# Gate products of a dense expert stage run on GpSimd between its row transfers instead of on VectorE

## The chip, the cores and the metric

One core of a Trainium2 chip runs the whole kernel, one launch. The metric is the device time in microseconds (us) of one execution; lower is better. TensorE multiplies matrices, VectorE and ScalarE work elementwise, GpSimd here issues DMA transfers and does a little elementwise work, SyncE only issues DMA.

## What is computed

Two layers of a diffusion backbone over 512 latent and 256 context tokens of width 1024. Each layer has a mixing part and then an expert part ("PEER"). Only the expert part is touched by the change:

```
def block(args):
    hb, eb, gb = args
    a = jnp.einsum('td,tkd->tk', hb, u_tab[eb])
    w = gb.astype(hb.dtype) * jax.nn.gelu(a, approximate=False)
    return jnp.einsum('tk,tkd->td', w, v_tab[eb])
```

Every token picks 128 of 16384 experts. Expert e has a row u and a row v; its gate times gelu(h . u) weights v in the output. The product `gb * gelu(a)` is what the change moves, for the tokens that are treated densely.

## The kernel before

It does the expert part in two ways at once. **Dense**: for most tokens (512 in layer 0, 384 in layer 1) it computes h . u for *all* 16384 experts as matmuls and multiplies by a gate matrix that is zero where a token didn't pick the expert. **Gathered**: for the remaining tokens (two groups of 128 in layer 0, one in layer 1) it fetches the picked rows of u and v by indirect DMA, 128 rows of 4 KB (one for each token) at a time, and treats them on VectorE.

The experts come in 128 tiles of 128, two tiles c = 0, 1 per *step* s, `NSUPER` = 64 steps a layer. fp32 accuracy is had by splitting each operand in a high and a low part (fp32r) and doing three matmuls for each product. In one step:

- TensorE does `apply_u` for step s+1 (48 matmuls, tile 0 and then tile 1, into PSUM banks psA 0 and 1) and then `apply_v` for step s (48 matmuls: four resident accumulators in psV, and four output chunks of 12 matmuls in turn, "cycled" through psA banks 2 and 3). The next step's `apply_u` follows. It waits for `hi_done` and `lo_done` (both parts of an expert tile's weights), for `w_ready` (both parts of the activations W) and for `cycled_free` (a cycled bank emptied).
- ScalarE takes gelu of u's result into `gel` (`gelu(c, s)`), then, after the product with the gates, makes `W_hi` (`high(c, s)`), and makes `split_hi` of the expert tiles.
- VectorE, in an order written out by hand in `experts`: `product(c, s)` (gel times gates, in place), `low(c, s)` (`W_lo` = gel - W_hi), `split_one` (`split_lo` of an expert tile, four a step: the two v tiles of this step, then the two u tiles of step s+2), `add_cycled(q)` (adds a cycled bank into xT), and `rows_used` (the work on one gathered transfer: for u a multiply with a sum, L1925, for v a multiply and add into y_tok, L1930). `share` is the number of such row ops a step: 8 in layer 0, 4 in layer 1.
- GpSimd issues the gathers (`gather(u)`, L1012) into a ring of 7 buffers (`RING`) and once a step the load of the gate block for step s+2 (`load_gates`, L1002) into one of two slots. A gather waits until VectorE has used the row that was in its buffer; the gates load waits until both `W_lo` of the step are made (`w_ready`), since then the slot is read out.
- SyncE loads the expert tiles, 512 KB each, into four `raw` buffers; a load waits until both parts of the tile four back are split.

`gel` has one buffer for each c: `gelu(c, s+1)` waits for `low(c, s)`. Engines go through their own order strictly, so whatever stands behind a wait waits too.

Of the kernel before, what the change touches and what calls it, by code (L numbers as in the profile page):

```python
# [34 lines left out]
ALU = mybir.AluOpType  # L35
# [9 lines left out]
TB = 32  # L45
# [9 lines left out]
NSUPER = NK // 2  # L55
# [9 lines left out]
DENSE = ((NCTX, NLAT), (NCTX, NLAT - P))  # L65
# [10 lines left out]
def gate_blocks(layer):  # L76

    s, n = DENSE[layer]
    return s // TB, (s + n) // TB
# [48 lines left out]
def build_program(nc, mod_pairs, mod_tiles, tiles, x_in, consts, params, bmod, cond, arow, aws, bw, keys, lblog, rope, pu0, pu1, pv0, pv1, gates, out):  # L128
    sem_ctx = ExitStack()

    def semaphore(name):
        return sem_ctx.enter_context(nc.semaphore(name))
# [14 lines left out]
    product_ready = semaphore("product_ready")  # L147
# [4 lines left out]
    g_landed = (semaphore("g_landed0"), semaphore("g_landed1"))  # L152
# [76 lines left out]
    gelu_ready = semaphore("gelu_ready")  # L229
# [34 lines left out]
    def in_r(name, offset, shape, dt=F32):  # L264
        assert offset + int(np.prod(shape[1:])) * 4 <= nc.sbuf_usable_end - RB, name
        return place(name, shape, dt, RB + offset)
# [103 lines left out]
    gel = in_r("gel", 16384, [P, 2, NLAT])  # L370
    g_in = in_r("g_in", 20480, [P, 2, NLAT // TB, 2 * TB])
# [23 lines left out]
    def pick(l, u):  # L395

        part, j = PASSES[l][u // PICKS]
        return part, j, u % PICKS
# [540 lines left out]
    @block.gpsimd  # L939
    def _(pool):  # L940
        seen = Counts()
        for k in range(KD):
            pool.dma_start(xT[:, k, :], x_in[:, k, :]).then_inc(inputs_landed, 16)
        for dst, src in ((cst[:], consts), (par[:], params), (bm[:], bmod), (c_raw[:], cond), (lb[:, 0:2, :], lblog)):
            pool.dma_start(dst, src).then_inc(inputs_landed, 16)

        def a_weights(l):
            pool.dma_start(a_wsT[:], aws[l]).then_inc(aw_landed, 16)
            pool.dma_start(a_bias[:], arow[l, :, 0:256]).then_inc(aw_landed, 16)
            pool.dma_start(a_norm[:], arow[l, :, 256:512]).then_inc(aw_landed, 16)  # L950

        a_weights(0)
        for b in range(2):

            seen.n[g_stored[b]] = 16
        for l in range(DEPTH):

            pool.wait_ge(a_done, seen.upto(a_done))
            pool.memset(states[:], 0.0).then_inc(states_zero, 1)
            pool.wait_ge(c_done, seen.upto(c_done))  # L960
            pool.dma_start(bc[64:96], rope).then_inc(rope_landed, 16)
            pool.dma_start(w_uq[:], bw[l]).then_inc(bw_landed, 16)
            pool.wait_ge(mix_ready, seen.upto(mix_ready))
            pool.dma_start(keysT[:], keys[l]).then_inc(keys_landed, 16)

            tb0, tb1 = gate_blocks(l)
            pool.wait_ge(sel_copied, seen.upto(sel_copied, DENSE[l][1] // P))
            if l + 1 < DEPTH:
                a_weights(l + 1)
            base = 3 + l * (NLAT // TB) * GROUPS  # L970
            steps = (tb1 - tb0) // 2 - 1
            nc.gpsimd.tensor_copy(first_key[:, 0], idxT[:, 0, tb0 * TB + 2:tb0 * TB + 4]).then_inc(pool_chain, 1)

            def first_one_hots(i, last):

                for g in range(2 * GROUPS):

                    pool.wait_ge(oh_passed, seen.at(oh_passed, base + g - 2 + (2 * GROUPS * steps if last else 0)))
                    pool.wait_ge(pool_chain, seen.upto(pool_chain))
                    if not last:  # L980
                        t = i * (2 * TB) + (tb0 * TB + 4 * (g + 1) + 2)
                        nc.gpsimd.tensor_copy(first_key[:, (g + 1) % 4], idxT[:, 0, bass.ds(t, 2)]).then_inc(pool_chain, 1)
                    elif g < 2 * GROUPS - 1:
                        t = (tb1 - 2) * TB + 4 * (g + 1) + 2
                        nc.gpsimd.tensor_copy(first_key[:, (g + 1) % 4], idxT[:, 0, t:t + 2]).then_inc(pool_chain, 1)
                    for j in range(2):
                        ins = nc.gpsimd.tensor_scalar(onehot[:, g % 4, 0, 2 + j], iota, first_key[:, g % 4, j:j + 1], None,  # L987
                                                      ALU.is_equal)
                    ins.then_inc(oh_first, 1)

            with pool.Fori(0, steps) as i:
                seen.enter(i, {oh_passed: 2 * GROUPS, pool_chain: 2 * GROUPS})
                first_one_hots(i, False)
            seen.leave(steps)
            first_one_hots(None, True)

            for b in range(2):
                pool.wait_ge(g_stored[b], seen.upto(g_stored[b], 16 * (tb1 - tb0) // 2))

            def load_gates(s, slot):  # L1000

                return pool.dma_start(g_in[:, slot, 0:tb1 - tb0, :].rearrange("p b (i t) -> p b i t", i=2),  # L1002
                                     gates[tb0:tb1].rearrange("b p (s i) t -> s p b i t", i=2)[s])\
                    .then_inc(g_landed[slot], 16)

            def gather(u):

                part, j, e = pick(l, u)
                b = (UNIT0[l] + u) % RING
                if UNIT0[l] + u >= RING:  # L1010
                    pool.wait_ge(row_used, UNIT0[l] + u - RING + 1)
                nc.gpsimd.indirect_dma_start(rows[:, b, :], None, ((pu0, pv0), (pu1, pv1))[l][part],  # L1012
                                             bass.IndirectOffsetOnAxis(pick_i[:, j, e:e + 1], 0))\
                    .then_inc(rows_landed[b], 16)

            load_gates(0, 0)
            load_gates(1, 1)
            pool.wait_ge(picked, seen.upto(picked, len(GATHERED[l])))
            share = UNITS[l] // NSUPER
            for s in range(NSUPER):  # L1020
                for u in range(s * share, (s + 1) * share):
                    gather(u)
                pool.wait_ge(w_ready, seen.upto(w_ready, 2))
                if s + 2 < NSUPER:
                    load_gates(s + 2, s % 2)
        pool.wait_ge(x_ready, seen.upto(x_ready, 1 + 2 * DEPTH))
        pool.dma_start(out, xT[:, :, NCTX:T]).then_inc(out_stored, 16)
        pool.wait_ge(out_stored, 16)
# [392 lines left out]
    def _(dve):  # L1421
        seen = Counts()
        seen.n[psum_V_free] = 4
        V = nc.vector
# [456 lines left out]
        def experts(l):  # L1881
            s0, n = DENSE[l]
            unit = [0]
            share = UNITS[l] // NSUPER

            def product(c, s):

                dve.wait_ge(gelu_ready, 2 + (l * NSUPER + s) * 2 + c + 1)
                if c == 0:
                    dve.wait_ge(g_landed[s % 2], seen.upto(g_landed[s % 2], 16))  # L1890
                g3 = gel[:, c, 0:n].rearrange("p (b t) -> p b t", t=TB)
                V.tensor_tensor(g3, g3, g_in[:, s % 2, 0:n // TB, c * TB:(c + 1) * TB], ALU.mult).then_inc(product_ready, 1)  # L1892

            def low(c, s):

                dve.wait_ge(whi_ready, seen.upto(whi_ready))
                V.tensor_tensor(W_lo[:, s % 2, c, 0:n], gel[:, c, 0:n], W_hi[:, s % 2, c, 0:n].bitcast(F32),  # L1897
                                ALU.subtract).then_inc(w_ready, 1)
# [33 lines left out]

            extra = share == 8
            dve.wait_ge(htok_ready, seen.upto(htok_ready))
            product(0, 0)
            low(0, 0)
            split_to(EX0[l] + 4)
            for s in range(NSUPER):
                base = splits[0]
                product(1, s)  # L1940
                rows_used(1)
                low(1, s)
                split_to(min(base + 1, EX0[l] + EXPERT_TILES))
                if extra:
                    rows_used(1)
                split_to(min(base + 2, EX0[l] + EXPERT_TILES))
                if s + 1 < NSUPER:
                    product(0, s + 1)
                rows_used(1)
                if s + 1 < NSUPER:  # L1950
                    low(0, s + 1)
                if extra:
                    rows_used(1)
                add_cycled(0)
                rows_used(1)
                add_cycled(1)
                split_to(min(base + 3, EX0[l] + EXPERT_TILES))
                if extra:
                    rows_used(1)
                add_cycled(2)  # L1960
                rows_used(1)
                split_to(min(base + 4, EX0[l] + EXPERT_TILES))
                if extra:
                    rows_used(1)
                add_cycled(3)
# [209 lines left out]
```

## Time and profile before

| | us |
|---|---|
| median of 3 runs | 5521.78 (5520.38 to 5523.92) |
| the profiled execution's own time | 5521.46 |
| its span, first to last instruction | 5519.6 |
| busy: TensorE / VectorE / ScalarE / GpSimd | 4585.9 / 3738.2 / 1635.1 / 1408.4 |
| expert stage of layer 0 | about 1814 to 3233 |
| expert stage of layer 1 | about 4422 to 5511 |
| granted TensorE clock, mean of the span | 0.872 of full speed |

Busy time says how much of the span an engine's instructions cover. For an end-to-end time one asks which wait ends last in a stage; an engine's idle time matters only if the others wait for what it does next. In the timelines a row's first number is the start from the span's start, the second the busy time, the third the engine, and a bracket tells how long the engine had been idle before and what ended it. The busy times of neighbours can overlap by some hundredths, so the place that an instruction takes in an engine's order is the difference of two starts.

### The profile page before, as it was taken

The page shows a single profiled execution, that of the slowest core. Times are in us where ns is not written, and L with a number is a line of the kernel's source. Part 1 is how long each engine was busy: PE and PEld are TensorE (multiplying, and loading weights), DVE is VectorE, ACT ScalarE, POOL GpSimd, SP SyncE. Part 2 cuts the span into 40 slices and gives each one's busy share as a digit, 9 for nine tenths or more (in the row PEclk, how much of TensorE's full clock was granted, in tenths as well). Part 3 has the DMA queues.
Part 4 walks back from the last instruction along what each step waited for, and adds up shares of the span by engine and source line. Part 5 has one row for each costly group of instructions (what it writes and reads, how often), then busy time and mean ns, then how long its engine had stood idle before and what let it go on. Part 6 is the DMA issues. An engine that isn't in the chain of part 4 may idle for free. (4 is left out here: it accounts for less than half of the span.)

```text
span 5519.6 us, 73901 instructions
## 1 busy us (share of the span) xinstructions
PE 4585.9 (83%) x24885; PEld 3932.6 (71%) x24885; DVE 3738.2 (68%) x7426; ACT 1635.1 (30%) x2249; POOL 1408.4 (26%) x1600
## 2 busy tenths in 40 slices
PE   5956599988627999999999978557782799999998
PEld 4956377776516788888888857534462699999998
DVE  1157322235999788889989952733469978888887
ACT  1221233322114322322322322234420333333332
POOL 0000000000029544544444410000000933333332
PEclk9965577779859999999999989568796999999999
DMA  3100022221104899999999931000010377778876
GB/s 123 58 1 1 15 84 84 84 88 35 39 35 175 286 316 312 313 317 311 314 315 311 314 117 39 1 15 0 20 65 23 166 254 281 275 271 280 278 270 230
DMA packets 232170, 898.96 MB, mean 163 GB/s; under 512 B 26160, under 2 KB 26192, under 8 KB 226656
## 3 DMA queue, kind: packets, MB, share of 16 engines
q0 software_dynamic: 129440, 474.96, 25.2%
q1 hardware_dynamic: 102528, 421.57, 21.6%
q8 instruction: 94, 1.54, 0.1%
q14 instruction: 108, 0.88, 0.1%
HBM read 835.61 MB, written 60.82 MB: 162 GB/s over the span
## 5 line engine op out<-in xcount | busy, mean ns | idle before, releaser
L414 PE MATMUL psA<-h_hi,split_hi 128*128 128x512 f32 (+2 forms) x2816 | 1017.5, 361 | 109.4 <-DVE h_lo L1452 64.6
L414 PE MATMUL psA<-h_lo,split_hi 128*128 128x512 f32 (+2 forms) x2816 | 1013.2, 360 | 0.0
L414 PE MATMUL psA<-h_hi,split_lo 128*128 128x512 f32 (+2 forms) x2816 | 1012.9, 360 | 0.0
L1434 DVE TENSOR_TENSOR split_lo<-raw,split_hi 128x1024 fp32r<-128x1024 f32 x596 | 727.2, 1220 | 225.8 <-ACT split_hi L1046 215.8
L1046 ACT ACTIVATE split_hi<-raw 128x1024 fp32r<-128x1024 f32 x596 | 629.9, 1057 | 90.8 <-PE psV L414 76.2
L414 PEld LDWEIGHTS psA<-h_hi,split_hi 128*128 128x128 f32 x2816 | 532.8, 189 | 172.7 <-DVE h_lo L1452 66.3
L1361 ACT ACTIVATE W_hi<-gel 128x512 fp32r<-128x512 f32 (+1 forms) x256 | 148.4, 580 | 1496.5 <-DVE gel L1892 1496.5
L414 PEld LDWEIGHTS psA<-h_hi,split_lo 128*128 128x128 f32 x2816 | 532.5, 189 | 60.3
L414 PEld LDWEIGHTS psA<-h_lo,split_hi 128*128 128x128 f32 x2816 | 532.9, 189 | 59.1
L1012 POOL DMA_INDIRECT rows<-pv,pick_i x384 | 458.1, 1193 | 405.6 <-DVE y_tok L1930 345.3
L1902 DVE SCALAR_TENSOR_TENSOR xT<-psA,mod,xT 128x512 f32<-128x512 f32 (+1 forms) x512 | 349.8, 683 | 306.5 <-PE psA L414 304.3
L1012 POOL DMA_INDIRECT rows<-pu,pick_i x384 | 455.6, 1187 | 390.5 <-DVE pick_a L1925 349.4
L1930 DVE SCALAR_TENSOR_TENSOR y_tok<-rows,pick_w,y_tok 128x1024 f32<-128x1024 f32 x381 | 487.2, 1279 | 3.6
L1925 DVE CUSTOM_DVE_ANT_1 rows<-rows,h_tok 128x1024 f32<-128x1024 f32 x384 | 468.0, 1219 | 3.3
L414 PE MATMUL psV<-W_hi,split_hi 128*128 128x512 f32 (+1 forms) x1024 | 371.6, 363 | 9.1 <-DVE W_lo L1897 9.1
L414 PE MATMUL psV<-W_hi,split_lo 128*128 128x512 f32 (+1 forms) x1024 | 371.2, 363 | 0.0
L414 PE MATMUL psV<-W_lo,split_hi 128*128 128x512 f32 (+1 forms) x1024 | 371.2, 363 | 0.0
L414 PE MATMUL psA<-W_hi,split_hi 128*128 128x512 f32 (+1 forms) x1024 | 370.8, 362 | 0.0
L414 PE MATMUL psA<-W_hi,split_lo 128*128 128x512 f32 (+1 forms) x1024 | 370.8, 362 | 0.0
L414 PE MATMUL psA<-W_lo,split_hi 128*128 128x512 f32 (+1 forms) x1024 | 370.8, 362 | 0.0
L414 PE MATMUL psA<-onehot 128*128 128x128 f32 x1792 | 260.6, 290 | 75.3 <-POOL onehot L987 43.2
L414 PE MATMUL psV<-lvl_q,lvl_k 64*64 64x64 f32 x2080 | 209.1, 315 | 123.3 <-DVE attF L1604 95.6
(274 smaller groups left out, 7596.7 us busy)
## 6 DMA issues: line engine op xcount, KB each, us to landing
raw<-tiles SPq DMA_DIRECT2D x596, 512.0 KB, 5.2
gates<-g_buf SPq DMA_DIRECT2D x28, 2048.0 KB, 6.4
raw<-mod_tiles SPq DMA_DIRECT2D x80, 512.0 KB, 3.2
g_in<-gates POOLq DMA_DIRECT2D x64, 512.0 KB, 9.3
g_in<-gates POOLq DMA_DIRECT2D x64, 384.0 KB, 5.9
mod_w<-mod_pairs SPq DMA_DIRECT2D x8, 1024.0 KB, 17.9
rows<-pu,pick_i POOLq DMA_INDIRECT x384, 7.4
rows<-pv,pick_i POOLq DMA_INDIRECT x384, 7.2
```

The source lines that it names most:

```text
L414: ins = nc.tensor.matmul(out_, lhsT, rhs, start=start, stop=stop)
L1012: nc.gpsimd.indirect_dma_start(rows[:, b, :], None, ((pu0, pv0), (pu1, pv1))[l][part], bass.IndirectOffsetOnAxis(pick_i[:, j, e:e + 1], 0))\
L1046: A(split_hi[:, n % SPLIT].rearrange("p k n -> p (k n)"), raw[:, n % RAW, :], ACT.Copy).then_inc(hi_done, 1)
L1361: A(W_hi[:, s % 2, c, 0:n], gel[:, c, 0:n], ACT.Copy).then_inc(whi_ready, 1)
L1434: V.tensor_tensor(split_lo[:, n % SPLIT].rearrange("p k n -> p (k n)"), raw[:, n % RAW, :], split_hi[:, n % SPLIT].rearrange("p k n -> p ( ...
L1902: return V.scalar_tensor_tensor(xT[:, k, s0:s0 + n], ps, mod[:, l * 48 + 40 + k, 0:1], xT[:, k, s0:s0 + n], ALU.mult, ALU.add)
L1925: ins = V.tensor_tensor_reduce(row, row, h_, 1.0, 0.0, ALU.mult, ALU.add, pick_a[:, j, e:e + 1])
L1930: ins = V.scalar_tensor_tensor(y_, row, pick_w[:, j, e:e + 1], y_, ALU.mult, ALU.add)
```

## The change

`product` leaves VectorE's order and goes to GpSimd's, with the same waits (gelu done, gates landed) and the same signal (`product_ready`, for ScalarE's `high`). On GpSimd, product(1, s) stands at the head of a step, and product(0, s+1) in the middle of the step's gathers.

```diff
+            def product(c, s):
+
+                n = DENSE[l][1]
+                pool.wait_ge(gelu_ready, 2 + (l * NSUPER + s) * 2 + c + 1)
+                if c == 0:
+                    pool.wait_ge(g_landed[s % 2], seen.upto(g_landed[s % 2], 16))
+                g3 = gel[:, c, 0:n].rearrange("p (b t) -> p b t", t=TB)
+                nc.gpsimd.tensor_tensor(g3, g3, g_in[:, s % 2, 0:n // TB, c * TB:(c + 1) * TB], ALU.mult).then_inc(product_ready, 1)
+
             load_gates(0, 0)
             load_gates(1, 1)
             pool.wait_ge(picked, seen.upto(picked, len(GATHERED[l])))
             share = UNITS[l] // NSUPER
+            product(0, 0)
             for s in range(NSUPER):
-                for u in range(s * share, (s + 1) * share):
+                product(1, s)
+                for u in range(s * share, s * share + share // 2):
+                    gather(u)
+                if s + 1 < NSUPER:
+                    product(0, s + 1)
+                for u in range(s * share + share // 2, (s + 1) * share):
                     gather(u)
                 pool.wait_ge(w_ready, seen.upto(w_ready, 2))
                 if s + 2 < NSUPER:
...
             dve.wait_ge(htok_ready, seen.upto(htok_ready))
-            product(0, 0)
             low(0, 0)
             split_to(EX0[l] + 4)
             for s in range(NSUPER):
                 base = splits[0]
-                product(1, s)
                 rows_used(1)
                 low(1, s)
...
                 split_to(min(base + 2, EX0[l] + EXPERT_TILES))
-                if s + 1 < NSUPER:
-                    product(0, s + 1)
                 rows_used(1)
```

GpSimd's instructions in a step of layer 1, before (L1002 loads gates, L1012 gathers rows):

```order
L1012 DMA rows<-pv,pick_i 128x1024 x4
L1002 DMA g_in<-gates 128x12x64
L1012 DMA rows<-pv,pick_i 128x1024 x4
L1002 DMA g_in<-gates 128x12x64
L1012 DMA rows<-pv,pick_i 128x1024 x4
```

And with the change (L1023 is the product):

```order
L1002 DMA g_in<-gates 128x12x64
L1023 TENSOR_TENSOR gel<-gel,g_in 128x384
L1012 DMA rows<-pv,pick_i 128x1024 x2
L1023 TENSOR_TENSOR gel<-gel,g_in 128x384
L1012 DMA rows<-pv,pick_i 128x1024 x2
L1002 DMA g_in<-gates 128x12x64
```

The four gathers of a step are now in two pairs, each behind a product. At the start of layer 0's stage, the piece of the difference on GpSimd:

```order
 L1002 DMA g_in<-gates 128x16x64 x2
-L1012 DMA rows<-pu,pick_i 128x1024 x8
-L1002 DMA g_in<-gates 128x16x64
+L1023 TENSOR_TENSOR gel<-gel,g_in 128x512 x2
+L1012 DMA rows<-pu,pick_i 128x1024 x4
+L1023 TENSOR_TENSOR gel<-gel,g_in 128x512
+L1012 DMA rows<-pu,pick_i 128x1024 x4
+L1002 DMA g_in<-gates 128x16x64
```

The first gathers stand behind product(0, 0) and product(1, 0). VectorE in one step of layer 1, before (L1902 is `add_cycled`, L1930 the row op, L1434 the split):

```order
L1892 TENSOR_TENSOR gel<-gel,g_in 128x384
L1930 SCALAR_TENSOR_TENSOR y_tok<-rows,pick_w,y_tok 128x8x128
L1897 TENSOR_TENSOR W_lo<-gel,W_hi 128x384
L1434 TENSOR_TENSOR split_lo<-raw,split_hi 128x1024 x2
L1892 TENSOR_TENSOR gel<-gel,g_in 128x384
L1930 SCALAR_TENSOR_TENSOR y_tok<-rows,pick_w,y_tok 128x8x128
L1897 TENSOR_TENSOR W_lo<-gel,W_hi 128x384
L1902 SCALAR_TENSOR_TENSOR xT<-psA,mod,xT 128x384
L1930 SCALAR_TENSOR_TENSOR y_tok<-rows,pick_w,y_tok 128x8x128
L1902 SCALAR_TENSOR_TENSOR xT<-psA,mod,xT 128x384
L1434 TENSOR_TENSOR split_lo<-raw,split_hi 128x1024
```

And with the change (lines moved by 7 to 15; L1937 is the row op, L1904 `low`, L1449 the split, L1909 `add_cycled`):

```order
L1937 SCALAR_TENSOR_TENSOR y_tok<-rows,pick_w,y_tok 128x8x128
L1904 TENSOR_TENSOR W_lo<-gel,W_hi 128x384
L1449 TENSOR_TENSOR split_lo<-raw,split_hi 128x1024 x2
L1937 SCALAR_TENSOR_TENSOR y_tok<-rows,pick_w,y_tok 128x8x128
L1904 TENSOR_TENSOR W_lo<-gel,W_hi 128x384
L1909 SCALAR_TENSOR_TENSOR xT<-psA,mod,xT 128x384
L1937 SCALAR_TENSOR_TENSOR y_tok<-rows,pick_w,y_tok 128x8x128
L1909 SCALAR_TENSOR_TENSOR xT<-psA,mod,xT 128x384
L1449 TENSOR_TENSOR split_lo<-raw,split_hi 128x1024
```

Nothing else moved: VectorE's rest closes up. TensorE's, ScalarE's and SyncE's orders are the same.

## Rows read from the trace of the kernel before

**Rows 1.** Windows: busy us (instructions) of each engine, granted TensorE clock, DMA share, GB/s
```profile
core 0: us, PE busy (x) PEld busy (x) DVE busy (x) ACT busy (x) POOL busy (x), PEclk, DMA share, GB/s
4909.15:4925.79 16.64, 16.64 (x98) 16.64 (x97) 13.72 (x21) 6.06 (x8) 6.08 (x5) 1.00 0.79 272
2203.25:2224.97 21.72, 21.72 (x97) 18.02 (x96) 19.33 (x29) 6.50 (x8) 10.64 (x9) 1.00 0.92 313
5495.60:5500.40 4.80, 4.80 (x15) 4.80 (x16) 1.68 (x3) 0.00 (x0) 0.00 (x0) 0.50 0.00 0
```

**Rows 2.** TensorE's waits in the stages of layers 0 and 1: total, times, longest
```profile
PE psA L414 <- ACT split_hi L1046: 6.8, 1, 6.8
PE psV L414 <- DVE W_lo L1897: 5.3, 1, 5.3
...
PE psA L414 <- DVE split_lo L1434: 10.1, 1, 10.1
PE psV L414 <- DVE W_lo L1897: 3.9, 1, 3.9
```

**Rows 3.** Timeline of VectorE in a step of layer 1: start, busy us
```profile
4910.80 0.55 DVE L1892 TENSOR_TENSOR gel<-gel,g_in 128x384 f32<-128x384 f32 x1
4911.26 1.22 DVE L1925 CUSTOM_DVE_ANT_1 rows<-rows,h_tok 128x1024 f32<-128x1024 f32 x1
...
4913.05 2.48 DVE L1434 TENSOR_TENSOR split_lo<-raw,split_hi 128x1024 fp32r<-128x1024 f32 x2
...
4919.75 0.62 DVE L1902 SCALAR_TENSOR_TENSOR xT<-psA,mod,xT 128x384 f32<-128x384 f32 x1 [2.01 <-PE psA L414]
4920.28 1.22 DVE L1925 CUSTOM_DVE_ANT_1 rows<-rows,h_tok 128x1024 f32<-128x1024 f32 x1
...
4921.83 0.62 DVE L1902 SCALAR_TENSOR_TENSOR xT<-psA,mod,xT 128x384 f32<-128x384 f32 x1 [0.32 <-PE psA L414]
4922.36 1.22 DVE L1434 TENSOR_TENSOR split_lo<-raw,split_hi 128x1024 fp32r<-128x1024 f32 x1
```

**Rows 4.** Timeline of VectorE in a step of layer 0
```profile
2205.95 0.68 DVE L1892 TENSOR_TENSOR gel<-gel,g_in 128x512 f32<-128x512 f32 x1
2206.55 1.22 DVE L1925 CUSTOM_DVE_ANT_1 rows<-rows,h_tok 128x1024 f32<-128x1024 f32 x1
...
2210.85 1.22 DVE L1434 TENSOR_TENSOR split_lo<-raw,split_hi 128x1024 fp32r<-128x1024 f32 x1
...
2217.71 1.22 DVE L1925 CUSTOM_DVE_ANT_1 rows<-rows,h_tok 128x1024 f32<-128x1024 f32 x1
```

**Rows 5.** Groups of GpSimd's instructions: busy us, mean ns, idle before
```profile
L987 POOL TENSOR_SCALAR onehot<-cst,first_key 128x128 f32<-128x128 f32 x448 | 301.8, 683 | 0.4
...
L982 POOL COPY first_key<-idxT 128x2 f32 x192 | 36.9, 192 | 0.5 <-POOL first_key L972 0.5
```

**Rows 6.** Timeline of GpSimd in the same step of layer 1
```profile
4913.26 1.07 POOL L1002 DMA_DIRECT2D g_in<-gates  x1 [9.34 <-DVE W_lo L1897]
4914.63 1.75 POOL L1012 DMA_INDIRECT rows<-pu,pick_i  x1 [0.30 <-issue]
...
4918.38 0.94 POOL L1012 DMA_INDIRECT rows<-pu,pick_i  x1 [0.30 <-issue]
```

**Rows 7.** Timeline of ScalarE in the same step: the gelu of tile 1
```profile
4917.66 0.49 ACT L1356 ACTIVATE gel<-psA 128x384 f32<-128x384 f32 x1 [0.98 <-PE psA L414]
```

**Rows 8.** Landing of the 218 gathers of layer 1, 4500 to 5400 us
```profile
DMA to landing us min/median/max: 6.5/7.3/8.8
```

**Rows 9.** Landing of one gather of layer 0, issued at 2201.43
```profile
DMA to landing us min/median/max: 5.3/5.3/5.3
```

**Rows 10.** Timeline of GpSimd and VectorE at the start of layer 0's stage
```profile
1823.67 1.04 POOL L1012 DMA_INDIRECT rows<-pu,pick_i  x1 [0.30 <-issue]
...
1827.67 0.69 DVE L1892 TENSOR_TENSOR gel<-gel,g_in 128x512 f32<-128x512 f32 x1 [16.20 <-DMA g_in<-gates]
...
1833.71 1.22 DVE L1925 CUSTOM_DVE_ANT_1 rows<-rows,h_tok 128x1024 f32<-128x1024 f32 x1
```

**Rows 11.** Head of the page
```profile
span 5519.6 us, 73901 instructions
```

More of the change, by code:

```diff
@@ L1884, in experts @@
             share = UNITS[l] // NSUPER
[L1886 to L1892, printed above, removed]
             def low(c, s):
```

## The prediction

> **What bounds the kernel now.** I read the windows first. In a stretch of one step of either expert stage TensorE is busy for all of it at a granted clock of 1.00 (16.64 of 16.64 us in layer 1, 21.72 of 21.72 in layer 0), VectorE for 13.72 and 19.33 us [rows 1]. TensorE's waits in the two stages come next: four of more than 1 us for expert matmuls, 6.8 and 5.3 us in layer 0, 10.1 and 3.9 in layer 1 [rows 2], all at a stage's start or end, since each came once. So 64 steps of 21.72 us and 64 of 16.64 run at TensorE's pace. VectorE's timeline comes third: its wait inside a step is on TensorE (2.01 us, [rows 3]), so relief for it gives nothing by itself. What counts is by how much each hand-over beats TensorE, and whether the new order keeps that.
>
> I count from T, the first h_hi matmul of a step's apply_u, where the windows begin (4909.15 and 2203.25 us). A step has 96 matmuls, so in layer 1 each takes 16.64 / 96 = 0.173 us: the first expert tile of apply_u is done at T+4.16, the second at T+8.32, then comes apply_v, and the next step begins at T+16.64. In layer 0 (0.226 us each) it is T+5.43, T+10.86 and T+21.72.
>
> **What is removed.** 256 products on VectorE, two in each of 128 steps. In layer 1 one takes 4911.26 - 4910.80 = 0.46 us of VectorE's order [rows 3], in layer 0 2206.55 - 2205.95 = 0.60 [rows 4]; together 2 x 64 x (0.46 + 0.60) = 136 us of an engine that waits for TensorE anyway. Worth inside the steps: 0.
>
> **What a product costs on GpSimd.** No row shows one. From below: VectorE's own 0.55 us of busy time for 384 elements [rows 3]. From above: GpSimd's TENSOR_SCALAR on 128 elements takes 683 ns and its copy of 2 elements 192 [rows 5], so (683 - 192) / 126 = 3.9 ns an element, 1.7 us for 384 and 2.2 for 512. I take the middle, 1.1 us for 384 and 1.4 for 512. The Trainium skill (GPSIMD Engine Reference, Performance versus the Vector engine) gives 4497 ns for a two-input op on 2048 elements; by it 512 elements would be near 1.15 us and 384 near 0.9 (an estimate), and layer 1's loss below would be 0.2 us a step smaller. No run here shows it yet.
>
> **GpSimd waits for VectorE.** The gather issued at 4914.63 took 1.75 us, the one at 4918.38 0.94 [rows 6]. At the first, VectorE was in its pair of splits (4913.05, 2.48 us, to 4915.53 [rows 3]), which ended 0.90 us after that start: 0.94 + 0.81 = 1.75. At the second VectorE stood idle. So a GpSimd instruction that reads SBUF is held while VectorE runs an op with two SBUF inputs, and a product will be too. Whether it holds VectorE in turn the trace doesn't show.
>
> **Layer 1, where I expect the loss.** Now GpSimd does the gates load at 4913.26 = T+4.11 and then four gathers in a row from 4914.63 on [rows 6], for the *next* step: what VectorE calls row 2 (its third row op of a step) is gathered over 16 us before its use. In the new order the second pair of gathers stands behind product(0, s+1), which needs gelu(0, s+1), and that can't come before TensorE has finished tile 0 of this step. The other gelu starts at 4917.66 = T+8.51, 0.19 after its tile's end, and takes 0.49 [rows 7]; so this one starts at T+4.35 and ends at T+4.84. VectorE is then in its pair of splits, which end at T+6.38 now and 0.46 earlier without product(1), T+5.92. Held until then, the product ends at T+7.02, and with some 0.3 us of issue the gather of row 2 starts at T+7.3. It is for *this* step.
>
> VectorE wants row 2 at 4920.28 = T+11.13 [rows 3]. Behind it stand add(1) at 4921.83, 0.33 us after the row's end (4920.28 + 1.22), and the split that ends at 4922.36 + 1.22 = T+14.43; TensorE wants that tile at T+16.64. The slack is 2.2 + 0.3 = 2.5 us, so the row may land until T+13.6. Gathers of this stage take 6.5 to 8.8 us to land, median 7.3 [rows 8]; one of layer 0 took 5.3 [rows 9]. With 7.3 it lands at T+14.6, with 6.5 at T+13.8, with 5.3 at T+12.6. The gates load no longer runs just ahead of it, but the two tile loads that the splits set off still do: I take 6.9 us, T+14.2, **0.6 us late per step**. Times 62 full steps: **+37 us**. Bounds: 0, and with 8.8 us 2.5 us a step (155 us). The pair's second row starts about 1.24 us later and is wanted some 4 us later, so it adds nothing. Product(1, s+1) is off the path: its gelu is done at T+9, and what follows from it was made only just before the next step's splits, T+3.9.
>
> **Layer 0.** VectorE is 89% busy, and gathers wait for a free one of 7 row buffers. The same sum: gelu done near 5.43 + 0.19 + 0.65 (0.49 scaled to 512) = T+6.3, half a row op of holding (0.6), product 1.4, issue 0.3: gather of row 4 at T+8.6. One of this layer landed in 5.3 us [rows 9]: T+13.9, or 14.6 with a hold of the gather; wanted at 2217.71 = T+14.46 [rows 4]. On time, just. The tighter chain is VectorE's own: it reaches the end of its second split of the v tiles at 2210.85 + 1.22 = T+8.8 [rows 4] and TensorE wants it at T+10.86: margin 2.1 us. Against it stand -0.6 (product(1) gone), +1.4 if product(0) holds VectorE and +0.7 for half of product(1): +1.5. It fits with 0.6 us over. Zero at best; where both products hold VectorE for 2.2 us, 3.8 - 2.1 = 1.7 us a step. For the steps where it doesn't fit I put 0.15 us each: **+10 us**.
>
> **Starts and ends.** At each stage's start product(0,0) costs 0.7 and 0.5 us more on a path that TensorE waits on. The first gather, issued at 1823.67 now, comes behind product(1,0): gates landed 1827.67 [rows 10] + 1.4 + two ScalarE ops of 0.65 + 1.4 + 0.3 = 1832.1, landing 7.3 later at 1839.4, where the row was used at 1833.71 [rows 10], 5.7 late. W_lo(1,0) and two splits stand behind it. A step's margins take 2 us each in the row's and the split's part; between 0 and 5.7 I take +1.5 in all. With the products +3 to +4. At the ends product(1,63) leaves VectorE's queue ahead of the last W_lo, which TensorE awaits (5.3 and 3.9 us, [rows 2]): -1. Net **+3**.
>
> **Sum.** 37 + 10 + 3 = 50 us on the profiled execution's 5521.5 us (span 5519.6 [rows 11], 1.9 around it; the runs' median is 5521.8): **5571 us**. A measurement of this kernel can tell about 0.2%, 11 us, from no change.
>
> **Rivals.**
> - *Hidden* (no change): rows land by T+13.6 in layer 1. It needs a landing within 6.3 us, or a product that isn't held (gather at T+6.2, landing at T+13.1). For it: the 5.3 us in layer 0. Against: this stage's landings were all 6.5 or more. Then only starts and ends are left: 5524 us. Chance 0.25.
> - *The products hold VectorE and are long*: 2.2 and 1.7 us, held both ways. Layer 0 loses 1.7 us a step (109 us), layer 1 0.6 + 0.6 for the longer product (74 us): with the ends 5707 us; at half of what that is above the forecast, 5639. For it: the stretched gather in [rows 6]. Against: VectorE's ops show no such stretch beside the gathers. Chance 0.12. The Trainium skill (SBUF — State Buffer, Who interferes with whom) has it as a rule: a VectorE instruction with two SBUF inputs contends with a GpSimd one that reads SBUF, and whoever is first has the shared port for its whole length. [rows 6] agree for the one direction (0.81 us of waiting); for the other no row here speaks.
> - *Faster*: the lighter VectorE ends the two end waits for W_lo (5.3 and 3.9 us) altogether, and TensorE then doesn't fall to half clock behind them (0.50 for 4.80 us after the last, [rows 1]; 2.4 us lost each time): -14 us, 5508. It decides if W_lo(1,63) is ready as apply_v(62) ends and no row is late. Against: a row op still stands ahead of that W_lo. Chance 0.05.
> - *Forecast*, rows late by tenths in layer 1: 0.58, own range 5535 to 5640.
>
> **Numbers.** Slower holds the forecast and the long products, 0.70; within 0.2% is the hidden case, 0.25; faster 0.05. Range 5519 (hidden, with the ends gaining) to 5665 (landings near 8.4 us in layer 1, 2.1 us a step, or more than half of the long products).
>
> **What the profile of the changed kernel would show.** GpSimd TENSOR_TENSOR near 1.1 us (384), stretched when it starts inside a VectorE split. In layer 1 VectorE's third row op of a step waiting for the rows' DMA near T+14, and TensorE then waiting for split_lo or xT, some tenths each step; a step of 17.2 us; rows landing 6.9 us after issue. In layer 0 steps of 21.7 to 21.9. I am wrong if layer 1's steps keep 16.64 us, if TensorE waits for W_lo instead, or if VectorE's ops are stretched or spaced by whole products.

## The result and the profile after

The changed kernel takes 5541.61 us (median of 5 executions; before 5522.85, median of 6). A sixth execution took 7921.99 us at a granted clock of 0.549 and is left out; with it the median would be 5543.18. The ratio is 1.0034 with a 95% interval of 1.002 to 1.0048: **slower, by 19 us**. I had said slower, by 49 us. The profiled execution took 5532.81 us; it is some 7 us earlier than the one of before when layer 0's stage begins, in code that nobody touched, so lengths of stages are compared here, not spans.

Windows of the two traces from each stage's first expert matmul of `apply_u` to the last of `apply_v`, answering to [rows 1]. The kernel before:

```profile
1814.00:3222.30 1408.30, 1396.27 (x6144) 1155.23 (x6144) 1248.49 (x1535) 417.25 (x515) 679.62 (x576) 1.00 0.91 311
4422.10:5506.10 1084.00, 1070.02 (x6143) 1069.44 (x6144) 881.73 (x1150) 387.41 (x512) 380.43 (x320) 0.99 0.78 270
```

The changed kernel (the columns are the stretch, its length, busy us and instructions of TensorE, its weight loads, VectorE, ScalarE and GpSimd, clock, DMA share, GB/s):

```profile
span 5531.0 us, 73966 instructions
...
1807.60:3218.10 1410.50, 1398.36 (x6143) 1156.98 (x6144) 1272.33 (x1407) 423.85 (x516) 958.75 (x704) 0.99 0.89 310
4414.90:5517.30 1102.40, 1082.77 (x6142) 1066.16 (x6143) 860.20 (x1022) 394.12 (x513) 569.51 (x448) 0.99 0.79 266
```

Layer 1's stage grew by 18.4 us, layer 0's by 2.2, together 20.6, which is the 19 us of the runs within their scatter. VectorE (the third busy figure) was relieved of 128 products of 0.69 us in layer 0, 88 us, and is busy for 24 us *more*. In layer 1 it was relieved of 128 x 0.55 = 70 us, and its busy time fell by only 21.5.

TensorE's waits in the two stages, answering to [rows 2]:

```profile
PE psA L414 <- ACT split_hi L1061: 7.2, 1, 7.2
PE psV L414 <- DVE W_lo L1904: 4.8, 1, 4.8
...
PE psA L414 <- DVE split_lo L1449: 10.6, 1, 10.6
PE psV L414 <- DVE W_lo L1904: 3.6, 1, 3.6
...
PE psA L414 <- DVE xT L1909: 2.0, 4, 1.1
```

The four waits at starts and ends are within 0.5 us of before. New is the last row. It is small, since the busy times of neighbouring matmuls overlap and cover most of a short delay: for the same matmuls TensorE's busy time in layer 1 grew from 1070.02 to 1082.77 us. GpSimd's product, in windows inside layer 0 and layer 1 (duration in ns, min/median/max):

```profile
L1023 POOL TENSOR_TENSOR gel<-gel,g_in x124: 1292/1790/2359, 1857.0 to 3192.4; 128x512 f32<-128x512 f32 x124
...
L1023 POOL TENSOR_TENSOR gel<-gel,g_in x124: 1010/1054/1989, 4458.3 to 5497.3; 128x384 f32<-128x384 f32 x124
```

Layer 1's median stands between two kinds: product(0, s+1), which starts at T+5.06 beside VectorE's splits, takes 1.79 us (median), and product(1, s+1), which starts at T+11.13, takes 1.04.

And the groups that waited for the gathers in layer 1, 4500 to 5400 us:

```profile
who waited for it (us, times):
  DVE rows L1932: 64.2, 28
  DVE y_tok L1937: 55.3, 25
...
DMA to landing us min/median/max: 5.3/6.2/8.1
```

In before no VectorE instruction waited for a row there. The worst step of layer 1 (its T is 4589.89; the next comes 18.38 us later) shows the chain. GpSimd, VectorE and the landing of the gather issued at 4596.89:

```profile
4594.95 1.80 POOL L1023 TENSOR_TENSOR gel<-gel,g_in 128x384 f32<-128x384 f32 x1 [7.39 <-ACT gel L1371]
4596.89 1.78 POOL L1012 DMA_INDIRECT rows<-pu,pick_i  x1
...
4601.02 1.03 POOL L1023 TENSOR_TENSOR gel<-gel,g_in 128x384 f32<-128x384 f32 x1
...
4594.65 3.17 DVE L1449 TENSOR_TENSOR split_lo<-raw,split_hi 128x1024 fp32r<-128x1024 f32 x2
...
4605.02 1.23 DVE L1932 CUSTOM_DVE_ANT_1 rows<-rows,h_tok 128x1024 f32<-128x1024 f32 x1 [3.84 <-DMA rows<-pu,pick_i]
4606.18 0.61 DVE L1909 SCALAR_TENSOR_TENSOR xT<-psA,mod,xT 128x384 f32<-128x384 f32 x1
4606.71 1.22 DVE L1449 TENSOR_TENSOR split_lo<-raw,split_hi 128x1024 fp32r<-128x1024 f32 x1
...
DMA to landing us min/median/max: 8.1/8.1/8.1
```

The product that starts 0.30 us into VectorE's pair of splits takes 1.80 us; the one that meets no such neighbour takes 1.03. The pair takes 3.17 us where it took 2.48 [rows 3]: each has held the other. The gather of row 2 starts at T+7.00, lands 8.1 us later at T+15.1, and VectorE has stood for 3.84 us. Behind the row op come `add_cycled(1)`, for whose bank TensorE waits, and the split of the next u tile. This is the late gather of the prediction.

Over all the full steps of layer 1, with the landing taken as the last of a gather's 16 completions: row 2's gather starts at T+7.00 (median), lands 6.60 us later (5.89 to 8.11), at T+13.51 (median, at most T+15.11). Where it lands before T+13.0 a step stays at 16.64 us or is at most 0.11 longer; where it lands late, step length minus 16.64 equals landing minus T+13.33 (median, 13.22 to 13.38). In layer 0 the steps stay at 21.76 us, as before (one of 21.85).

### The profile page after: what moved, and what is told of

Same layout as the page of the kernel before. It is cut to its first block and busy times, and to the rows that moved or that the text cites. A ratio compares the mean times of both kernels' runs of the same rounds, so it can differ in the third digit from the quotient of the medians.

```text
span 5531.0 us, 73966 instructions
## 1 busy us (share of the span) xinstructions
PE 4596.0 (83%) x24885; PEld 3927.1 (71%) x24885; DVE 3737.7 (68%) x7170; ACT 1648.5 (30%) x2249; POOL 1873.4 (34%) x1856
## 3 DMA queue, kind: packets, MB, share of 16 engines
q1 hardware_dynamic: 102528, 421.57, 21.7%
## 5 line engine op out<-in xcount | busy, mean ns | idle before, releaser
L1449 DVE TENSOR_TENSOR split_lo<-raw,split_hi 128x1024 fp32r<-128x1024 f32 x596 | 828.5, 1390 | 216.8 <-ACT split_hi L1061 213.8
L1023 POOL TENSOR_TENSOR gel<-gel,g_in 128x512 f32<-128x512 f32 (+1 forms) x256 | 403.5, 1576 | 748.0 <-ACT gel L1371 739.4
L1937 DVE SCALAR_TENSOR_TENSOR y_tok<-rows,pick_w,y_tok 128x1024 f32<-128x1024 f32 x381 | 516.4, 1355 | 77.5 <-DMA rows<-pv,pick_i 71.4
L1932 DVE CUSTOM_DVE_ANT_1 rows<-rows,h_tok 128x1024 f32<-128x1024 f32 x384 | 486.5, 1267 | 88.6 <-DMA rows<-pu,pick_i 82.4
L1012 POOL DMA_INDIRECT rows<-pv,pick_i x384 | 491.4, 1280 | 98.0 <-issue 91.4
L1012 POOL DMA_INDIRECT rows<-pu,pick_i x384 | 486.4, 1267 | 97.7 <-issue 90.3
L1909 DVE SCALAR_TENSOR_TENSOR xT<-psA,mod,xT 128x512 f32<-128x512 f32 (+1 forms) x512 | 349.4, 682 | 178.5 <-PE psA L414 173.4
```

The source lines that it names most:

```text
L1023: nc.gpsimd.tensor_tensor(g3, g3, g_in[:, s % 2, 0:n // TB, c * TB:(c + 1) * TB], ALU.mult).then_inc(product_ready, 1)
L1449: V.tensor_tensor(split_lo[:, n % SPLIT].rearrange("p k n -> p (k n)"), raw[:, n % RAW, :], split_hi[:, n % SPLIT].rearrange("p k n -> p ( ...
L1909: return V.scalar_tensor_tensor(xT[:, k, s0:s0 + n], ps, mod[:, l * 48 + 40 + k, 0:1], xT[:, k, s0:s0 + n], ALU.mult, ALU.add)
L1932: ins = V.tensor_tensor_reduce(row, row, h_, 1.0, 0.0, ALU.mult, ALU.add, pick_a[:, j, e:e + 1])
L1937: ins = V.scalar_tensor_tensor(y_, row, pick_w[:, j, e:e + 1], y_, ALU.mult, ALU.add)
```

## The experiments

Each was timed beside the kernel before on the same chip, so the time of before differs a little from one to the next. Steps and stages are read from each one's trace. Where I split a stage in three, the start part runs from its first `apply_u` matmul to the first T that follows an `apply_v`, the end part from the last T to the last matmul, and the steps lie between.

**e1: the product behind all four gathers.** GpSimd's order, on the changed kernel:

```diff
                 product(1, s)
-                for u in range(s * share, s * share + share // 2):
-                    gather(u)
-                if s + 1 < NSUPER:
-                    product(0, s + 1)
-                for u in range(s * share + share // 2, (s + 1) * share):
+                for u in range(s * share, (s + 1) * share):
                     gather(u)
+                if s + 1 < NSUPER:
+                    product(0, s + 1)
```

> The changed kernel, with the product of tile 0 of the next step issued behind all four row gathers of the step instead of between the second and the third; the product still runs on GpSimd, as many times, and the same work is done. Late gather (my theory): layer 1's loss of 18.4 us comes only from the gather of row 2, which starts at about T+6.9 behind the held product. With it issued directly behind row 1, it lands before VectorE asks for it, the steps of layer 1 go back to 16.64 us, VectorE's third row operation no longer waits for a DMA, and the total is 5521 to 5527 us (0 to 4 us over the kernel before). The split of tile 0's low half now waits for a product that comes up to two gathers later (3.6 us): if that costs more than its slack of some 5 us, TensorE waits for split_lo. Rival, the shared SBUF path: the loss is the longer splits on VectorE (3.17 us a pair instead of 2.48 us) and the product's place doesn't matter: steps stay at about 16.95 us and the total at 5540 to 5545 us.

Measured: 5517.64 us against 5519.89, ratio 0.9996 (0.9987 to 1.0005), no change that can be told. Every step of layer 1 is 16.64 us, its stage 1081.6. Row 2 starts before T (T-3.1) and lands at T+5.2 (median). The total is 3 us below my range: layer 1's end part takes 28.8 us where it took 31.6 before, and I have no experiment on why. GpSimd and VectorE in one step of e1:

```profile
4899.71 1.64 POOL L1023 TENSOR_TENSOR gel<-gel,g_in 128x384 f32<-128x384 f32 x1 [4.23 <-ACT gel L1369]
...
4900.52 1.92 DVE L1930 CUSTOM_DVE_ANT_1 rows<-rows,h_tok 128x1024 f32<-128x1024 f32 x1
...
4905.34 0.62 DVE L1907 SCALAR_TENSOR_TENSOR xT<-psA,mod,xT 128x384 f32<-128x384 f32 x1 [2.42 <-PE psA L414]
4905.87 1.21 DVE L1930 CUSTOM_DVE_ANT_1 rows<-rows,h_tok 128x1024 f32<-128x1024 f32 x1
```

The mutual holding is still there: a row op beside the product takes 1.92 us, its like elsewhere 1.21. But VectorE still waits 2.42 us for TensorE behind it, so it costs nothing. It is the place of the gather that costs here, not the product's presence.

**e2: layer 1's products back on VectorE**, at their old places; layer 0's stay on GpSimd (`product` of each engine is guarded by `l`).

> The changed kernel with the products of layer 1 back on VectorE at their old places; layer 0's products stay on GpSimd, before and between its gathers. The same work is done. Theory: the whole loss is layer 1's, since layer 0's steps measured 21.76 us in both traces; total 5521 to 5527 us, layer 0's stage about 2 us longer than before, layer 1's steps at 16.64 us. Rival, both layers pay (the two layers' shares as I forecast, 10 to 37, or a cost in layer 0 that the steps hide and its ends show): 5527 to 5533 us.

Measured: 5521.93 us, ratio 1.0 (0.9991 to 1.0009). Layer 1's stage is 1084.2 us (before 1084.0), layer 0's 1410.5 (before 1408.3, changed kernel 1410.5). The loss is layer 1's but for 2 us, as expected.

**e3: the late gather without the product.** The kernel before, with one wait on GpSimd:

```diff
                 for u in range(s * share, (s + 1) * share):
+                    if l == 1 and u == s * share + share // 2 and s + 1 < NSUPER:
+                        pool.wait_ge(product_ready, (l * NSUPER + s) * 2 + 3)
                     gather(u)
```

> The kernel before, products on VectorE, with one wait more: in layer 1 the gather of row 2 (and row 3 behind it) waits until VectorE has made the product of tile 0 of the next step. GpSimd computes no product. The same work is done. Late gather: the gather now starts when VectorE's product has ended, about T+7 or somewhat later, so layer 1 loses as much as in the changed kernel or more: steps of 16.9 to 17.6 us, 17 to 60 us in all, VectorE's third row operation waiting for a DMA at about T+13.5. Rival, the shared SBUF path: without a product on GpSimd nothing holds VectorE, and the steps stay at 16.64 us with a total within 4 us of before.

Measured: 5609.8 us against 5519.89, ratio 1.0157 (1.0143 to 1.0171), 90 us slower, beyond the 17 to 60 that I expected. Waits of TensorE and of VectorE in its layer 1:

```profile
PE psA L414 <- DVE xT L1904: 49.7, 57, 1.7
...
DVE y_tok L1932 <- DMA rows<-pv,pick_i: 109.2, 31, 4.3
DVE rows L1927 <- DMA rows<-pu,pick_i: 106.7, 31, 4.2
```

GpSimd computes nothing here, so nothing holds VectorE; yet VectorE waits for the third row in every step. VectorE makes the product behind both of its splits, so row 2's gather starts at T+8.75 (median) and lands at T+14.83. The landing limit read from its steps is T+13.33, the same as in the changed kernel. 14.83 - 13.33 = 1.5 us, times 61 steps is 92 us: the stage grew by 1173.5 - 1084.0 = 89.5. One number, the landing against T+13.33, tells the lengths of both kernels.

**e7: the product one gather later** than in the changed kernel, ahead of row 3 instead of row 2 (`share // 2` becomes `share * 3 // 4` in both loops).

> The changed kernel with the product of tile 0 of the next step one gather later: in layer 1 between the third and the fourth gather, in layer 0 between the sixth and the seventh. The same work is done. Theory: in layer 1 only the gather of row 3 is behind the held product now; it starts at T+7 and lands at about T+13.5, and in the changed kernel row 3 landed at T+15.3 without a wait of its own. Row 2 lands in front of T+7. So layer 1's steps are back at 16.64 us and the total is 5516 to 5524 us. Rival: row 3 is wanted before T+13.5 when VectorE isn't late any more, and steps grow by 0.1 to 0.3 us: 5525 to 5540 us.

Measured: 5521.48 us against 5521.37, ratio 1.0 (0.9991 to 1.0009); every step 16.64 us, stage 1084.3, as expected. So one gather's place is the whole loss of layer 1. Row 3 can stand behind the product.

**e6 and e8: more holding.** e1 with k more two-input operations of 384 elements behind each product of layer 1, on a constant tile into a scratch tile (`scr`); k = 1 in e6, 2 in e8.

```diff
+                for i in range(k if l == 1 and s < NSUPER - 1 else 0):
+                    nc.gpsimd.tensor_tensor(scr[:, c * 3 + i], resets[:, 0:384], resets[:, 0:384], ALU.mult)
```

> e1 with one more two-input product of 384 elements behind each product of layer 1 on GpSimd (it multiplies a constant tile by itself into a scratch tile that nobody reads or waits for; the outputs are unchanged). In e1 a product beside VectorE's operations lengthens one of them by 0.70 us (a row operation of 1.92 us instead of 1.21 us), and VectorE waits for TensorE for 3.1 us a step. Theory (the hold is paid from VectorE's slack, only gathers that land late cost time): two holds more take up to 1.4 us of the 3.1 us, gathers start 1 to 2 us later and still land by T+8, far from T+13.3: steps stay at 16.64 us, the total within 5 us of e1 (5513 to 5523 us). Rival (the hold is on the path): 2 x 0.7 us a step or 90 us more, 5600 us; half of it 5560 us.

Measured for e6: 5526.52 us, ratio 1.0009 (1.0 to 1.0018). All steps are 16.64 us. The 5 us over before are not in the steps: layer 1's stage is 1089.0 us against e1's 1081.6, of which the start part took 6.1 us (44.2 against 38.1) and the end part 1.4. The total is 3.5 us above my range. VectorE's low split in e1 and then in e6, 4600 to 5400 us (busy us, mean ns):

```profile
L1902 DVE TENSOR_TENSOR W_lo<-gel,W_hi 128x384 fp32r<-128x384 f32 x96 | 52.7, 549 | 0.0
```

```profile
L1905 DVE TENSOR_TENSOR W_lo<-gel,W_hi 128x384 fp32r<-128x384 f32 x96 | 82.8, 862 | 0.0
```

An instruction that ran free now loses 0.31 us on average to the added work, two of them a step, and the steps don't mind. That is half of the 1.4 us of holding that I had expected the added work to bring, so e6 tests the rival with 0.6 us a step and not with 1.4.

> e6 with two more products instead of one behind each of layer 1 (scratch results, outputs unchanged). GpSimd is then busy for 10.0 us (e1) + 4 x 1.0 to 1.6 us = 14 to 16.4 us of a step of 16.64 us, and VectorE's slack of 3.1 us has 2.8 us of holds to pay. Theory: at the edge, steps of 16.64 to 17.3 us, 5515 to 5560 us, and if time is lost, the rows' landing or GpSimd's own length shows it. Rival (each hold of 0.7 us is on the path): 4 x 0.7 us a step, about 5690 us.

Measured for e8: 5629.12 us, ratio 1.0197 (1.0183 to 1.021), between what the two theories gave and outside both. TensorE's main wait in its layer 1, one of VectorE's pairs of splits, and the window of the stage:

```profile
PE psV L415 <- DVE split_lo L1450: 81.8, 32, 6.2
...
4749.49 5.49 DVE L1450 TENSOR_TENSOR split_lo<-raw,split_hi 128x1024 fp32r<-128x1024 f32 x2
...
4420.90:5626.30 1205.40, 1108.61 (x6143) 1097.36 (x6144) 1037.66 (x1022) 393.94 (x513) 896.16 (x700) 0.95 0.73 243
```

VectorE is busy for 1037.66 / 64 = 16.2 us a step, the step's whole 16.64 us but for 0.4, and the pair of splits takes 5.49 us where it took 2.48. Nearly every fourth step is 20 to 25 us long, the others 16.6 to 17.7. So holding cost no step anything while VectorE had slack (e1, e6), and with the slack used up steps are lost. But rows come late here as well (VectorE waited 69 us for them in layer 1), and GpSimd is itself busy for 896.16 / 64 = 14.0 us a step; which of them starts the long steps is not separated.

**e4, e9, e10, e5: the ends of the stages.** From the kernel before; e4 has both edits, e9 the first alone, e10 the second alone. With the second, step 63 leaves out the product and the low split that step 62 has made. ScalarE's part of the first makes four `split_hi` ahead of the first two gelus and two more behind them, ahead of the first `W_hi`.

```diff
+            split_to(EX0[l] + 6)
             product(0, 0)
             low(0, 0)
-            split_to(EX0[l] + 4)
             for s in range(NSUPER):
-                base = splits[0]
+                base = EX0[l] + 4 + 4 * s
...
+                if s == NSUPER - 2:
+                    product(1, s + 1)
                 add_cycled(0)
                 rows_used(1)
                 add_cycled(1)
+                if s == NSUPER - 2:
+                    low(1, s + 1)
```

> The kernel before, products on VectorE, with the order at the two ends of each layer's expert stage changed: both engines split six weight tiles of the first step ahead of the gelu and the product instead of four behind them (and stay two tiles further ahead in the steps), and the product and the low split of tile 1 of the last step are made one step earlier, around the second row operation of the step before the last. The same work is done. Theory: TensorE's waits of the stage's start and end (6.8 us for split_hi and 5.3 us for W_lo in layer 0, 10.1 us and 3.9 us in layer 1) shrink by half or more, some of it at half clock: 10 to 25 us faster, 5497 to 5513 us. Rival: those waits are set by the first gelu and by weight transfers, and the extra splits only move the wait to the product: within 4 us of before.

> The kernel before with only the start part of e4: six weight tiles of the first step split ahead of the first gelu's copy and product, and both engines two tiles further ahead in the steps; the last step is unchanged. The same work is done. Before, TensorE waits at the starts 6.8 us (split_hi, layer 0) and 10.1 us (split_lo, layer 1), and runs at half clock behind each. Theory: the start is the larger part of e4's 23 us: 14 to 18 us faster, 5502 to 5508 us. Rival: being two tiles further ahead fills the last step too, and this part alone gives all of it, 5496 to 5500 us.

> The kernel before with only the end part of e4: product and low split of tile 1 of the last step made one step earlier. The same work is done. Before, TensorE waits for W_lo 5.3 us at layer 0's end and 3.9 us at layer 1's. Theory: these 9.2 us less about 2 to 4 us that stay (e4 still has 1.5 and 2.4 us of waits there): 5 to 8 us faster, 5512 to 5518 us. Rival: the wait passes to the split of the last weight tiles, which VectorE makes behind the row operations either way: within 3 us of before.

Measured: e4 5496.91 us, ratio 0.9955 (0.9941 to 0.9968), **23 us faster than before**; e9 5506.19, 0.9972 (0.9961 to 0.9983); e10 5511.77, 0.9982 (0.9973 to 0.9991). The parts add up: 0.28% + 0.18% against 0.45%. e4 is at the fast edge of my range, e9 within it, e10 just under it. The waits left in e4's layer 1:

```profile
PE psV L414 <- DVE W_lo L1898: 2.4, 1, 2.4
PE psA L414 <- ACT gel L1356: 2.1, 1, 2.1
```

and the first 38 us of layer 1's stage, in the kernel before and in e4:

```profile
4422.00:4460.00 38.00, 27.80 (x145) 27.51 (x146) 15.88 (x23) 10.74 (x15) 12.69 (x11) 0.87 0.75 260
```

```profile
4409.90:4447.90 38.00, 33.26 (x189) 32.65 (x190) 23.04 (x32) 14.36 (x20) 17.72 (x14) 1.00 0.88 284
```

In e4 the 10.1 us wait of [rows 2] is gone, the granted clock is 1.00 instead of 0.87, and TensorE gets 189 matmuls done instead of 145.

e5 is e4's edits on e1, products on GpSimd:

> Two edits that passed apart, together: products on GpSimd with all four gathers ahead of the product of tile 0 (as in e1), and the order of splits, gelus, products and low splits at the ends of each stage from e4. The same work is done. Theory: the steps of both layers stay at 21.76 and 16.64 us, so the ends' gain of 23 us is kept whole: 5492 to 5500 us. VectorE has products less to do at the start, where GpSimd's product stands beside VectorE's splits, so a few us more may go or come: the side against is that the first product on GpSimd, held by VectorE's splits (1.8 us instead of 0.55), delays the first W_lo, 5500 to 5508 us.

Measured: 5510.77 us against 5521.37, ratio 0.9982 (0.9973 to 0.9991): faster than before, but it keeps less than half of e4's gain, and misses both my ranges. Its steps are 21.76 and 16.64 us; its stages are 7.5 and 6.1 us longer than e4's, all of it in the start parts (40.3 and 36.2 us against 32.8 and 30.2); the end parts are equal within 0.1 us. Its waits in layer 0 and in layer 1:

```profile
PE psA L414 <- DVE xT L1908: 3.8, 2, 3.0
PE psV L414 <- DVE W_lo L1903: 2.5, 1, 2.5
...
PE psV L414 <- DVE W_lo L1903: 4.1, 1, 4.1
PE psA L414 <- ACT gel L1369: 2.1, 1, 2.1
```

The start of layer 1's stage shows where the time goes. In e4 it begins at 4410.11, in e5 at 4415.03. GpSimd's first gather and VectorE's first row op in e4:

```profile
4422.55 1.77 POOL L1012 DMA_INDIRECT rows<-pu,pick_i  x1 [0.30 <-issue]
4430.07 1.23 DVE L1926 CUSTOM_DVE_ANT_1 rows<-rows,h_tok 128x1024 f32<-128x1024 f32 x1 [2.48 <-DMA rows<-pu,pick_i]
```

And in e5, with the two products ahead of the gather:

```profile
4430.29 1.98 POOL L1023 TENSOR_TENSOR gel<-gel,g_in 128x384 f32<-128x384 f32 x2 [3.15 <-DMA g_in<-gates]
4432.44 1.19 POOL L1012 DMA_INDIRECT rows<-pu,pick_i  x1 [0.16 <-issue]
...
4436.84 2.66 DVE L1931 CUSTOM_DVE_ANT_1 rows<-rows,h_tok 128x1024 f32<-128x1024 f32 x1 [4.15 <-DMA rows<-pu,pick_i]
```

The first gather starts 17.4 us into the stage instead of 12.4, since both products wait for the gates (3.15 us) ahead of it. VectorE stands 4.15 us for its row instead of 2.48, takes 2.66 us for the row op instead of 1.23, and low(1, 0) stands behind both. product(0, 0) itself is only some 0.5 us longer than VectorE's. So the late gather is in the start too; how the 7.5 and 6.1 us divide between it, the held row op and the longer products was not tested apart. e4 is the version that beats both kernels, and in it the product is on VectorE.

## Why the prediction was right in sign and too large

- **The mechanism of layer 1 was right.** Row 2 of a step lands late because its gather stands behind the held product, 18.4 of the 20.6 us. e7 and e1 remove it by place alone and e3 makes it without the product.
- **The step that failed is the size of layer 1's term: 0.6 us late a step, +37 us.** It measured 18.4 us, 0.3 us a step. The gather's start was put at T+7.3 and is T+7.00. The time to landing was put at 6.9 us and is 6.60. The limit was put at T+13.6 and is T+13.33. The first two bring the landing 0.7 us forward, to T+13.51, and the limit takes 0.3 back. That leaves 0.2 us late at the median; 38 of 61 landings come after even T+13.37, and the scatter (to T+15.11) makes the mean loss. A term that is the difference of a start near T+7, a landing near 7 and a limit near T+13.5 doubles or vanishes with 0.3 us of error in each.
- **How the product is held was half right.** I let it wait for the end of VectorE's pair of splits and had it end at T+7.02. In the worst step it ends at T+6.86, but the pair ends at T+7.93: the product got in between the two splits and pushed the second back. Both are stretched, not one.
- **Layer 0's +10 us did not come.** The landing forecast of row 4 was fair (T+13.9 to T+14.6 said, T+14.19 measured, wanted at T+14.46). The chain of VectorE was put at +1.5 us a step against 2.1 of margin, and by the windows VectorE loses (24 + 88) / 64 = 1.75 us to holding for 1.4 of relief. Every step but one of 21.85 us kept TensorE's pace, where I had allowed 0.15 us a step for misses.
- **Starts and ends, +3:** measured 2.1 in layer 0 and, with 61 steps' excess of 18.8 us taken from 18.4, -0.4 in layer 1: 1.7 in all.
- **The sign list.** Third row op waiting for DMA near T+14: yes (the worst at T+15.1). Step of 17.2 us: 16.95 mean. Layer 0 at 21.7 to 21.9: 21.76. Product of 1.1 us for 384 elements: 1.04 where nothing is beside it. I had taken the middle between two bounds that lay 1.2 us apart, so that this came out is partly luck. For 512 I said 1.4 and the median is 1.79, since there it is nearly always held (111 of 124 take over 1.5 us; the shortest 1.29).
- **The rivals.** *Hidden* needed every landing by T+13.6 as I had the limit, T+13.33 as measured, and 38 of 61 come after T+13.37. The price of *products hold VectorE and are long* was wrong, though half of its mechanism is real: they do hold VectorE, for 0.7 us a time, and e6 shows that nearly twice that holding costs no step anything. I had left open whether the product holds VectorE: it does. The Trainium skill (SBUF — State Buffer, Who interferes with whom) says it of both directions, and this case's rows agree: 1.80 us against 1.03 for the product, 3.17 against 2.48 for the pair. *Faster* did not come: the two end waits for W_lo went from 5.3 and 3.9 us to 4.8 and 3.6 only. e10 gets most of such a gain, 9.5 us, by making product(1, 63) and low(1, 63) earlier on VectorE.

## What to carry to other kernels

An elementwise operation moved into an engine that also issues transfers is priced by the transfers behind it: ask which of them becomes late, and by how much it beats its user. Here one place later in the queue made 20 us of loss into none. Relief of an engine that waits anyway gave no shorter step; and where instructions of the engine and its helper hold each other, as here, the relief may be given back in longer instructions. Where steps run at the bound engine's pace, look at the first and the last step: an order that is right for the loop left 23 us there (e4), and the start is where the products on GpSimd cost e5 most of that gain.

## What the runs showed of the hardware

- Moving 128 products of 0.69 us off VectorE made VectorE busier by 24 us in layer 0: its instructions beside GpSimd's products got longer, and the profile counts that time as busy.
- GpSimd's gathers and its products are not alike in this. A gather is stretched beside a split (1.75 to 1.8 us against 0.94), but VectorE's splits and row ops beside gathers stay at 1.22 us; only GpSimd's products stretched them.
- How long a gather takes to land differs with its place among those issued together: in e1's layer 1 the first of a step's four takes 4.35 us (median), the third 8.39. In the view of all of them, 4500 to 5400 us, e1 has:

```profile
DMA to landing us min/median/max: 4.2/6.6/9.4
```

One landing time for a stage, as my sum used from [rows 8], doesn't carry over to another order of issue.
